# Mixture-of-experts down products with the two bf16 halves of an expert's inner activations side by side

## The chip, the cores and the metric
The kernel runs on one core of one Trainium2 chip. The metric is device microseconds of that core for one launch. TensorE is called PE here, its weight loads PEld, VectorE DVE, ScalarE ACT, GpSimd POOL and SyncE SP.

## The reference
Two transformer-like blocks run on 512 tokens of width 1024. The first has a gated linear attention and a state-space mixer, and then product-key retrieval of experts. The second has a token mixer with attention, and then a hierarchical mixture of experts. Only the last part is touched here:

```
x_rows = hf[row_tok]                       # rows sorted by expert, 32 experts, top 2 of them a token
a = xb @ w_e_gate[e]                       # 1024 -> 512
u = xb @ w_e_up[e]                         # 1024 -> 512
y = (silu(a) * u) @ w_e_down[e]            # 512 -> 1024
out = x + sum over a token's two experts of y * weight, then rmsnorm
```

## The kernel before, in words
All weights stream from HBM in float32 chunks of 128 x 2048 (1 MB). Each chunk is split in two bf16 parts: ACT copies it to `w_hi` (`hi_of`, line 1686), and DVE subtracts that from the original into `w_lo` (`lo_of`, line 2369). Activations are split in the same way. A product is then three bf16 matmuls, high by high, high by low and low by high, summed in PSUM (`mm3`, lines 738 to 740).

The mixture of experts takes up to 64 rows (`CAP`) of each of 32 experts. An expert has six chunks: two for gate, two for up, two for down. `w_hi` and `w_lo` are rings of four chunks; the float32 chunks wait in a ring of twelve, which SP loads. On PE each chunk costs 12 matmuls of 512 columns. The program of an engine for one expert is its `step`, run in a loop of two steps; each engine works through its own list strictly in order, and semaphores tie the lists together. In step c:

- **PE**: gate of expert c (24 matmuls), transposes of expert c-1's inner activations (`expert_hidden`, line 1275, 8 small matmuls), transposes of the gathered rows of c+1 (`expert_rows`, line 1245, 16 small matmuls), down of c-1 (24 matmuls with 64 columns of weights in the array), up of c (24 matmuls).
- **ACT**: high part of the inner activations of c-1 (line 1699), one `hi_of`, Silu of the gate sums (line 1695), copy of the transposed inner activations out of PSUM (line 1703), copy of the high half of the transposed rows (line 1690), three `hi_of`, copy of the down sums (line 1708), two `hi_of`.
- **DVE**: low part of the inner activations of c-1 (line 2460), two `lo_of`, copy of the low half of the transposed rows (line 2451), three `lo_of`, Silu times up (line 2456), one `lo_of`.
- **POOL** gathers the rows of a later expert by indirect DMA and stores the outputs of c-1 to HBM.

The chunk of `hi_of(k + 4)`, the first that ACT splits after its copies, is the first chunk of up; the next one is up's second. Before a chunk may be split, PE must be done with the chunk four places earlier. After the last expert, POOL gathers every token's two output rows, and DVE and ACT weigh, add and normalise them.

Of the kernel before, what the change touches and what calls it, by code (L numbers as in the profile page):

```python
# [11 lines left out]
ALU = mybir.AluOpType  # L12
# [141 lines left out]
def build_program(nc, w_all, x_in, cols_in, small_in, rows_in, out):  # L154
    ctx = ExitStack()
    with ctx:  # L156
# [3 lines left out]
        def sem(name):  # L160
            return ctx.enter_context(nc.semaphore(name))
# [163 lines left out]
        hid_b = view(o, 2, DE, dt=BF16); o += DE  # L325
        hidT = view(o, 2, DE // P, CAP, dt=BF16); o += DE // P * CAP
        y_st = view(o, 2, D); o += 2 * D
# [101 lines left out]
        xe_ld = [sem(f"xe_ld{p}") for p in range(2)]  # L429
        xe_tp, xe_hi, xe_lo = sem("xe_tp"), sem("xe_hi"), sem("xe_lo")  # L430
        moe_ld = w_ld + [sem(f"moe_ld{s}") for s in range(RING, MOE_RING // 2)]
        moe_mm = sem("moe_mm")
        sil_done, hid_mul, hid_hi, hid_lo, hid_tp, hid_c = (sem(n) for n in ("sil_done", "hid_mul", "hid_hi", "hid_lo", "hid_tp", "hid_c"))
        y_out = sem("y_out")
        y_stored = [sem(f"y_stored{p}") for p in range(2)]
# [297 lines left out]
        def _(pe):  # L733
# [504 lines left out]
            def expert_rows(r, i, c):  # L1238

                pe.wait_ge(xe_ld[c % 2], 16 * (pairs_of(r, i, c) + 1))  # L1240
                wait(pe, xe_hi, moe(r, i, c))
                wait(pe, xe_lo, moe(r, i, c))
                for a in range(2):
                    for kt in range(KT):
                        last = pe.matmul(ps[:, 6 + a, kt * CAP:(kt + 1) * CAP], x_g[0:CAP, c % 2, a, kt * P:(kt + 1) * P],
                                         ident_b[0:CAP, 0:CAP], start=True, stop=True)
                    last.then_inc(xe_tp, 1)

            def expert_in(r, i, c, k, bank):

                for part in range(2):
                    chunk(C_MOE + r * PASS + 12 * i + (k + part))
                    for j in range(4):
                        kt, w = part * 4 + j, slice(j * DE, (j + 1) * DE)
                        last = mm3(ps[0:CAP, bank, :], xeT[:, c % 2, 0, kt, :], xeT[:, c % 2, 1, kt, :],
                                   w_hi[:, (k + part) % RING, w], w_lo[:, (k + part) % RING, w], kt == 0, kt == KT - 1)
                    last.then_inc(moe_mm, 1)

            def expert_gate(r, i, c):
                wait(pe, sil_done, moe(r, i, c))  # L1260
                pe.wait_ge(xe_hi, moe(r, i, c) + 1)
                pe.wait_ge(xe_lo, moe(r, i, c) + 1)
                expert_in(r, i, c, 6 * c - 2 if c else 0, 0)

# [4 lines left out]
            def expert_hidden(r, i, c):  # L1269

                pe.wait_ge(hid_lo, moe(r, i, c) + 1)
                for a in range(2):
                    for f in range(DE // P):
                        n = a * (DE // P) + f
                        last = pe.matmul(ps[:, 4, n * CAP:(n + 1) * CAP], hid_b[0:CAP, a, f * P:(f + 1) * P], ident_b[0:CAP, 0:CAP],
                                         start=True, stop=True)
                last.then_inc(hid_tp, 1)

            def expert_down(r, i, c, k):
                pe.wait_ge(hid_c, moe(r, i, c) + 1)  # L1280
                pe.wait_ge(y_out, moe(r, i, c) + 1)
                for part in range(2):
                    chunk(C_MOE + r * PASS + 12 * i + (k + part))
                    for half in range(2):
                        for j in range(2):
                            f, w = part * 2 + j, slice(j * D + half * 512, j * D + (half + 1) * 512)
                            last = mm3(ps[0:CAP, 2 + half, :], hidT[:, 0, f, :], hidT[:, 1, f, :],
                                       w_hi[:, (k + part) % RING, w], w_lo[:, (k + part) % RING, w], f == 0, f == DE // P - 1)
                    last.then_inc(moe_mm, 1)
# [12 lines left out]
            def step(r, i, c, more=True):  # L1302
                expert_gate(r, i, c)
                expert_hidden(r, i, c - 1)
                if more:
                    expert_rows(r, i, c + 1)
                expert_down(r, i, c - 1, 6 * c)
                expert_up(r, i, c)
# [12 lines left out]
        def _(act):  # L1321
# [365 lines left out]

            def rows_hi(r, i, c):
                act.wait_ge(xe_tp, 2 * moe(r, i, c) + 5)
                act.activation(xeT[:, c % 2, 0, :, :].rearrange("p k t -> p (k t)"), ps[:, 6, 0:KT * CAP], ACT.Copy).then_inc(xe_hi, 1)  # L1690

# [9 lines left out]
            def hidden_copy(r, i, c):  # L1701
                act.wait_ge(hid_tp, moe(r, i, c) + 1)
                act.activation(hidT.rearrange("p a f t -> p (a f t)"), ps[:, 4, 0:2 * DE // P * CAP], ACT.Copy).then_inc(hid_c, 1)  # L1703

            def outputs(r, i, c, k):
                act.wait_ge(moe_mm, r * PASS + 12 * i + (k + 2 + RING))
                act.wait_ge(y_stored[c % 2], 16 * (pairs_of(r, i, c) + 1))
                act.activation(y_st[0:CAP, c % 2, :].rearrange("p (b n) -> p b n", b=2), ps[0:CAP, 2:4, :], ACT.Copy).then_inc(y_out, 1)  # L1708

            def first(r):  # L1710
                if not isinstance(r, int):
                    for k in range(AHEAD):
                        hi_of(r, 0, k)
                rows_hi(r, 0, 0)
                hi_of(r, 0, 3)
                hi_of(r, 0, 4)
                silu(r, 0, 0, 0)
                rows_hi(r, 0, 1)
                hi_of(r, 0, 5)
                hi_of(r, 0, 6)  # L1720

            def step(r, i, c, more=True):
                k = 6 * c - 2
                hidden_hi(r, i, c - 1)
                hi_of(r, i, k + 3)
                silu(r, i, c, k)
                hidden_copy(r, i, c - 1)
                if more:
                    rows_hi(r, i, c + 1)
                hi_of(r, i, k + 4)  # L1730
# [27 lines left out]
        def _(dve):  # L1758
# [689 lines left out]

            def rows_lo(r, i, c):
                dve.wait_ge(xe_tp, 2 * moe(r, i, c) + 6)  # L2450
                dve.tensor_copy(xeT[:, c % 2, 1, :, :].rearrange("p k t -> p (k t)"), ps[:, 7, 0:KT * CAP]).then_inc(xe_lo, 1)

# [9 lines left out]
            def first(r):  # L2462
# [6 lines left out]
                lo_of(r, 0, 1)  # L2469
                rows_lo(r, 0, 0)  # L2470
                for k in range(2, 5):
                    lo_of(r, 0, k)
                rows_lo(r, 0, 1)
                lo_of(r, 0, 5)
# [3 lines left out]
            def step(r, i, c, more=True):  # L2478
# [3 lines left out]
                lo_of(r, i, k + 4)  # L2482
                if more:
                    rows_lo(r, i, c + 1)
                lo_of(r, i, k + 5)
                lo_of(r, i, k + 6)
                if more:
                    lo_of(r, i, k + 7)
# [3 lines left out]
            def last(r):  # L2492
                step(r, 0, NE - 1, more=False)
                hidden_lo(r, 0, NE - 1)

            one_pass = every_expert(first, step, last)
# [111 lines left out]
```

## Time and profile before

| | |
|---|---|
| median of 3 runs | 2748.45 us (2743.22 to 2752.5) |
| profiled execution | 2750.43 us |
| its span | 2748.8 us |
| mean granted clock of PE | 0.981 |
| PE busy | 2609.0 us, 95% |
| DVE busy | 1941.9 us, 71% |
| ACT busy | 1230.8 us, 45% |
| DMA, mean over the span | 224 GB/s |
| a weight load into `xn`, issue to landing, median of 32 | 9.2 us |

A matmul's busy time in the profile overlaps that of the next one, so the distance from start to start is what it costs. The same holds for the short ACT and DVE instructions: the next one starts about 0.1 us before the one before is shown to end. The step of one expert is best read as the distance between the same instruction of two neighbouring experts.

### The profile page before, as it was taken

Reading aid. Unit: us, or ns where it says so; the run is one execution under the profiler, and the core shown is the slowest. Engines: PE = TensorE matmul, PEld = TensorE weight load, DVE = VectorE, ACT = ScalarE, POOL = GpSimd, SP = SyncE. Lnnn points to the kernel's source line nnn. Section 1 sums busy time; section 2 is a strip of 40 time slices with the busy share of each in tenths; the row PEclk is TensorE's granted clock in tenths of the full one; section 3 lists DMA queues with packets and bytes.
Section 4 is the critical chain, followed back from the end, with each engine's and each line's share of the span. In section 5 each row is a group of like instructions: output and inputs, shape, how many; then the busy total and the mean of one; then the engine's idle time right before and its main releaser. Section 6 shows DMA issues by size and latency. Waiting matters only on the chain. (4 is left out here: it accounts for less than half of the span.)

```text
span 2748.8 us, 38654 instructions
## 1 busy us (share of the span) xinstructions
PE 2609.0 (95%) x13878; PEld 1321.1 (48%) x14069; DVE 1941.9 (71%) x3255; ACT 1230.8 (45%) x1316; POOL 945.4 (34%) x724
## 2 busy tenths in 40 slices
PE   8989999999999999999999899999999799999994
PEld 4465444444444444444444444555544455555552
DVE  6455887988855635888888754465534688888885
ACT  5434223223234432333333443444422588888883
POOL 0000000277777736888888200000001322222221
PEclk9989999999999999999999999999999799999997
DMA  5201874343436478999999532211123699999993
GB/s 215 108 16 58 291 279 177 125 160 139 176 142 162 154 188 286 365 367 363 368 366 363 195 123 107 82 72 62 62 77 138 244 391 395 394 393 394 403 408 139
DMA packets 175580, 614.83 MB, mean 224 GB/s; under 512 B 58336, under 2 KB 74720, under 8 KB 125792
## 3 DMA queue, kind: packets, MB, share of 16 engines
q1 hardware_dynamic: 57312, 411.62, 39.5%
q0 software_dynamic: 47712, 127.12, 12.7%
q10 hardware_dynamic: 70432, 74.46, 8.8%
q8 instruction: 76, 1.25, 0.2%
q14 instruction: 48, 0.39, 0.0%
HBM read 539.59 MB, written 73.53 MB: 223 GB/s over the span
## 5 line engine op out<-in xcount | busy, mean ns | idle before, releaser
L739 PE MATMUL ps<-a_lo,w_hi 128*128 128x512 bf16 (+2 forms) x1747 | 642.2, 370 | 4.2 <-issue 0.8
L740 PE MATMUL ps<-a_hi,w_lo 128*128 128x512 bf16 (+2 forms) x1745 | 641.4, 370 | 1.3 <-DVE xn L2314 0.2
L738 PE MATMUL ps<-a_hi,w_hi 128*128 128x512 bf16 (+2 forms) x1698 | 623.4, 370 | 9.1 <-ACT xn L1492 3.0
L738 PE MATMUL ps<-w_hi,arena 128*128 128x512 bf16 (+1 forms) x1582 | 604.1, 382 | 26.6 <-ACT arena L1703 14.6
L739 PE MATMUL ps<-w_lo,arena 128*128 128x512 bf16 (+1 forms) x1583 | 603.7, 381 | 0.9
L740 PE MATMUL ps<-w_hi,arena 128*128 128x512 bf16 (+1 forms) x1583 | 603.2, 381 | 0.9
L2019 DVE TENSOR_TENSOR w_lo<-w_st,w_hi 128x2048 bf16<-128x2048 f32 x127 | 290.5, 2289 | 222.3 <-ACT w_hi L1486 222.3
L1486 ACT ACTIVATE w_hi<-w_st 128x2048 bf16<-128x2048 f32 x127 | 242.4, 1908 | 338.4 <-PE ps L740 317.9
L624 POOL DMA_INDIRECT gate_dram<-arena x256 | 320.4, 1252 | 85.4 <-issue 79.4
L1492 ACT ACTIVATE xn<-ps 128x512 f32<-128x512 f32 x128 | 76.1, 596 | 440.9 <-PE ps L740 440.9
L738 PEld LDWEIGHTS ps<-a_hi,w_hi 128*128 128x128 bf16 x1768 | 173.5, 98 | 195.0 <-issue 10.9
L740 PEld LDWEIGHTS ps<-a_hi,w_lo 128*128 128x128 bf16 x1768 | 173.4, 98 | 194.7 <-issue 1.8
L738 PEld LDWEIGHTS ps<-w_hi,arena 128*128 128x128 bf16 (+1 forms) x1600 | 166.6, 104 | 208.5 <-issue 19.4
L639 POOL DMA_INDIRECT arena<-act_dram,h_idx x128 | 248.7, 1943 | 39.0 <-issue 39.0
L739 PEld LDWEIGHTS ps<-a_lo,w_hi 128*128 128x128 bf16 x1768 | 173.3, 98 | 181.7 <-issue 1.1
L740 PEld LDWEIGHTS ps<-w_hi,arena 128*128 128x128 bf16 (+1 forms) x1600 | 166.7, 104 | 181.6 <-issue 3.7
L739 PEld LDWEIGHTS ps<-w_lo,arena 128*128 128x128 bf16 (+1 forms) x1600 | 166.6, 104 | 176.8 <-issue 2.9
L1767 DVE TENSOR_TENSOR w_lo<-w_st,w_hi 128x2048 bf16<-128x2048 f32 x68 | 155.0, 2287 | 121.7 <-ACT w_hi L1330 121.5
L667 POOL CAST arena<-xn 128x1024 bf16<-128x1024 f32 x4 | 4.1, 1036 | 549.4 <-DVE xn L1781 549.4
L1330 ACT ACTIVATE w_hi<-w_st 128x2048 bf16<-128x2048 f32 x68 | 129.0, 1906 | 99.3 <-PE ps L740 98.0
L2369 DVE TENSOR_TENSOR w_lo<-w_st,w_hi 128x2048 bf16<-128x2048 f32 x64 | 146.0, 2282 | 28.1 <-ACT w_hi L1686 28.1
L689 POOL DMA_DIRECT2D y_dram<-arena x32 | 18.3, 573 | 389.5 <-ACT arena L1708 389.5
(406 smaller groups left out, 3803.5 us busy)
## 6 DMA issues: line engine op xcount, KB each, us to landing
w_st<-in_w_all SPq DMA_DIRECT2D x260, 1024.0 KB, 5.5
arena<-in_w_all SPq DMA_DIRECT2D x64, 1024.0 KB, 9.5
act_dram<-xn POOLq DMA_DIRECT2D x64, 512.0 KB, 3.0
xn<-in_w_all SPq DMA_DIRECT2D x32, 1024.0 KB, 9.2
arena<-act_dram ACTq DMA_DIRECT2D x64, 384.0 KB, 5.3
gate_dram<-xn ACTq DMA_DIRECT2D x14, 1536.0 KB, 8.4
arena<-gate_dram ACTq DMA_DIRECT2D x64, 336.0 KB, 7.2
a_hi<-in_w_all SPq DMA_DIRECT2D x16, 1024.0 KB, 8.9
```

What stands on the lines that cost most here:

```text
L624: pool.indirect_dma_start(gate_cells, bass.IndirectOffsetOnAxis(ap=place[:, b, j:j + 1], axis=0), shared[:, b, j:j + 1], None).then_inc(g_ ...
L639: pool.indirect_dma_start(act_0[:, k:k + 1], None, acts, bass.IndirectOffsetOnAxis(ap=h_idx[:, k:k + 1], axis=0)).then_inc(act_ld[k // ROW ...
L689: pool.dma_start(y_dram[moe(r, i, c)], y_st[0:CAP, c % 2, :]).then_inc(y_stored[c % 2], 16)
L738: pe.matmul(dst, l_hi, r_hi, start=start, stop=False)
L739: pe.matmul(dst, l_hi, r_lo, start=False, stop=False)
L740: return pe.matmul(dst, l_lo, r_hi, start=False, stop=stop)
L1330: act.activation(dst, w_st[:, n % RING, :], ACT.Copy).then_inc(w_hi_done, 1)
L1486: act.activation(w_hi[:, s, :], w_st[:, s, :], ACT.Copy).then_inc(w_hi_done, 1)
L1492: act.activation(u_st[:, n % 2, t, :], ps[:, t, :], ACT.Gelu).then_inc(u_out, 1)
L1767: dve.tensor_tensor(lo_n, w_st[:, n % RING, :], hi_n, ALU.subtract).then_inc(w_lo_done, 1)
L2019: dve.tensor_tensor(w_lo[:, s, :], w_st[:, s, :], w_hi[:, s, :], ALU.subtract).then_inc(w_lo_done, 1)
L2369: dve.tensor_tensor(w_lo[:, s, :], moe_st[k % MOE_RING], w_hi[:, s, :], ALU.subtract).then_inc(w_lo_done, 1)
```

## The change
The transposed inner activations `hidT` are laid out with the high and the low half of a block of 128 features side by side, 2 x 64 columns. One matmul with all 128 columns as weights and `w_hi` as the moving side gives high by high in PSUM partitions 0 to 63 and low by high in partitions 64 to 127. A second one with the high half alone and `w_lo` adds the third product to partitions 0 to 63. So a down chunk has 8 matmuls and no longer 12. ACT then copies partitions 64 to 127 to SBUF (`outputs`), and DVE adds partitions 0 to 63 to them (`outputs_add`, new, between its fourth and fifth `lo_of`).

The transposes of expert c-1's inner activations move on PE from behind the gate product of c to a place within it, ahead of its last three matmuls. On ACT their copy moves ahead of Silu. The two halves of the transposed rows, which ACT and DVE copied one each, are now copied by ACT in one instruction of 1024 columns (`rows_out`), which waits for all 16 transposes.

```diff
-            def expert_in(r, i, c, k, bank):
+            def expert_in(r, i, c, k, bank, within=None):
...
+                        if within and kt == KT - 1:
+                            within()
                         last = mm3(ps[0:CAP, bank, :], xeT[:, c % 2, 0, kt, :], xeT[:, c % 2, 1, kt, :],
...
# expert_hidden
-                        n = a * (DE // P) + f
+                        n = 2 * f + a
...
# expert_down
-                            last = mm3(ps[0:CAP, 2 + half, :], hidT[:, 0, f, :], hidT[:, 1, f, :],
-                                       w_hi[:, (k + part) % RING, w], w_lo[:, (k + part) % RING, w], f == 0, f == DE // P - 1)
+                            both = lambda start, stop: pe.matmul(ps[0:2 * CAP, 2 + half, :], hidT[:, f, :, :].rearrange("p a t -> p (a t)"),
+                                                                 w_hi[:, (k + part) % RING, w], start=start, stop=stop)
+                            rest = lambda: pe.matmul(ps[0:CAP, 2 + half, :], hidT[:, f, 0, :], w_lo[:, (k + part) % RING, w],
+                                                     start=False, stop=False)
+                            if f < DE // P - 1:
+                                both(f == 0, False)
+                                last = rest()
+                            else:
+                                rest()
+                                last = both(False, True)
...
# PE's step
-                expert_gate(r, i, c)
-                expert_hidden(r, i, c - 1)
+                expert_gate(r, i, c, lambda: expert_hidden(r, i, c - 1))
...
# ACT
-            def rows_hi(r, i, c):
-                act.wait_ge(xe_tp, 2 * moe(r, i, c) + 5)
-                act.activation(xeT[:, c % 2, 0, :, :].rearrange("p k t -> p (k t)"), ps[:, 6, 0:KT * CAP], ACT.Copy).then_inc(xe_hi, 1)
+            def rows_out(r, i, c):
+                act.wait_ge(xe_tp, 2 * moe(r, i, c) + 6)
+                act.activation(xeT[:, c % 2, :, :, :].rearrange("p a k t -> p a (k t)"), ps[:, 6:8, 0:KT * CAP], ACT.Copy).then_inc(xe_done, 1)
...
-                act.activation(y_st[0:CAP, c % 2, :].rearrange("p (b n) -> p b n", b=2), ps[0:CAP, 2:4, :], ACT.Copy).then_inc(y_out, 1)
+                act.activation(y_st[0:CAP, c % 2, :].rearrange("p (b n) -> p b n", b=2), ps[CAP:2 * CAP, 2:4, :], ACT.Copy).then_inc(y_low, 1)
...
# ACT's step
                 hi_of(r, i, k + 3)
+                hidden_copy(r, i, c - 1)
                 silu(r, i, c, k)
-                hidden_copy(r, i, c - 1)
                 if more:
-                    rows_hi(r, i, c + 1)
+                    rows_out(r, i, c + 1)
...
# DVE
-            def rows_lo(r, i, c):
-                dve.wait_ge(xe_tp, 2 * moe(r, i, c) + 6)
-                dve.tensor_copy(xeT[:, c % 2, 1, :, :].rearrange("p k t -> p (k t)"), ps[:, 7, 0:KT * CAP]).then_inc(xe_lo, 1)
+            def outputs_add(r, i, c):
+                dve.wait_ge(y_low, moe(r, i, c) + 1)
+                y = y_st[0:CAP, c % 2, :].rearrange("p (b n) -> p b n", b=2)
+                dve.tensor_tensor(y, ps[0:CAP, 2:4, :], y, ALU.add).then_inc(y_out, 1)
...
# DVE's step
                 hidden_lo(r, i, c - 1)
                 lo_of(r, i, k + 3)
                 lo_of(r, i, k + 4)
-                if more:
-                    rows_lo(r, i, c + 1)
                 lo_of(r, i, k + 5)
                 lo_of(r, i, k + 6)
+                outputs_add(r, i, c - 1)
                 if more:
                     lo_of(r, i, k + 7)
                 hidden(r, i, c, k + 4)
```

## Rows read from the trace of the kernel before

**Rows 1.** Busy time by stretch; columns: us, then each engine, PEclk, DMA share, GB/s.
```profile
2400.00:2500.00 100.00, 97.40 (x569) 50.69 (x568) 88.77 (x53) 83.32 (x66) 28.03 (x19) 1.00 1.01 393
```

**Rows 2.** Waits, 2200 to 2650 us; columns: us in total, times, longest us.
```profile
DVE w_lo L2369 <- ACT w_hi L1686: 50.5, 27, 1.9
```

**Rows 3.** Timeline of PE, one step; columns: start us, us, operation [idle before <-releaser].
```profile
2640.51 0.38 PE L740 MATMUL ps<-w_hi,arena 128*64 128x512 bf16 x1
2640.82 0.41 PE L1275 MATMUL ps<-ident_b,arena 64*128 64x64 bf16 x8
2641.06 0.63 PE L1245 MATMUL ps<-ident_b,arena 64*128 64x64 bf16 x16
2642.12 0.40 PE L738 MATMUL ps<-w_hi,arena 128*64 128x512 bf16 x1 [0.43 <-ACT arena L1703]
...
2659.08 0.40 PE L738 MATMUL ps<-w_hi,arena 128*64 128x512 bf16 x1 [0.43 <-ACT arena L1703]
```

**Rows 4.** Timeline of DVE, the same step.
```profile
2639.55 0.68 DVE L2460 TENSOR_TENSOR arena<-arena 64x512 bf16<-64x512 f32 x1
...
2644.30 2.29 DVE L2369 TENSOR_TENSOR w_lo<-w_st,w_hi 128x2048 bf16<-128x2048 f32 x1 [1.87 <-ACT w_hi L1686]
2646.51 0.69 DVE L2451 CAST arena<-ps 128x512 bf16<-128x512 f32 x1
2647.11 2.28 DVE L2369 TENSOR_TENSOR w_lo<-w_st,w_hi 128x2048 bf16<-128x2048 f32 x1
...
2653.72 0.67 DVE L2456 TENSOR_TENSOR arena<-arena,ps 64x512 f32<-64x512 f32 x1
2654.31 2.28 DVE L2369 TENSOR_TENSOR w_lo<-arena,w_hi 128x2048 bf16<-128x2048 f32 x1
2656.51 0.67 DVE L2460 TENSOR_TENSOR arena<-arena 64x512 bf16<-64x512 f32 x1
```

**Rows 5.** Timeline of ACT, the same step.
```profile
2640.92 0.59 ACT L1695 ACTIVATE arena<-ps 64x512 f32<-64x512 f32 x1 [1.03 <-PE ps L740]
2641.41 0.58 ACT L1703 ACTIVATE arena<-ps 128x512 bf16<-128x512 f32 x1
...
2642.37 3.70 ACT L1686 ACTIVATE w_hi<-w_st 128x2048 bf16<-128x2048 f32 x2
...
2647.77 1.01 ACT L1708 ACTIVATE arena<-ps 64x1024 f32<-64x1024 f32 x1
2648.67 1.91 ACT L1686 ACTIVATE w_hi<-arena 128x2048 bf16<-128x2048 f32 x1
```

**Rows 6.** Timeline of PE, the last expert.
```profile
2707.18 0.41 PE L1275 MATMUL ps<-ident_b,arena 64*128 64x64 bf16 x8 [3.65 <-DVE arena L2460]
2708.27 0.63 PE L738 MATMUL ps<-w_hi,arena 128*64 128x512 bf16 x1 [0.69 <-ACT arena L1703]
```

**Rows 7.** Timeline of DVE, the last expert.
```profile
2706.45 0.68 DVE L2460 TENSOR_TENSOR arena<-arena 64x512 bf16<-64x512 f32 x1
```

**Rows 8.** Timeline of ACT: expert 1's Silu, expert 31's, and the last output copy.
```profile
2183.01 0.59 ACT L1695 ACTIVATE arena<-ps 64x512 f32<-64x512 f32 x1 [1.97 <-PE ps L740]
...
2691.86 0.59 ACT L1695 ACTIVATE arena<-ps 64x512 f32<-64x512 f32 x1 [1.09 <-PE ps L740]
...
2715.36 1.02 ACT L1708 ACTIVATE arena<-ps 64x1024 f32<-64x1024 f32 x1 [7.14 <-PE ps L740]
```

**Rows 9.** Timeline of SP's queue: the last weight loads.
```profile
2677.86 0.86 SPq L560 DMA_DIRECT2D xn<-in_w_all  x2
```

**Rows 10.** Timeline of PE, attention stage: two long waits.
```profile
1514.73 0.39 PE L738 MATMUL ps<-w_hi,arena 128*128 128x512 bf16 x1 [2.45 <-DVE arena L2169]
...
1544.68 0.59 PE L738 MATMUL ps<-w_hi,arena 128*128 128x512 bf16 x1 [3.88 <-DVE arena L2169]
```

**Rows 11.** Busy time by stretch, after each of those waits.
```profile
1514.00:1520.00 6.00, 5.22 (x24) 2.44 (x26) 5.82 (x6) 1.12 (x2) 4.78 (x5) 1.00 0.87 316
1544.00:1548.00 4.00, 3.32 (x9) 1.28 (x10) 3.10 (x3) 0.68 (x1) 0.00 (x0) 0.57 0.72 262
```

More of the change, by code:

```diff
@@ L325, in build_program @@
         hid_b = view(o, 2, DE, dt=BF16); o += DE
-        hidT = view(o, 2, DE // P, CAP, dt=BF16); o += DE // P * CAP
+        hidT = view(o, DE // P, 2, CAP, dt=BF16); o += DE // P * CAP
         y_st = view(o, 2, D); o += 2 * D
@@ L429, in build_program @@
         xe_ld = [sem(f"xe_ld{p}") for p in range(2)]
-        xe_tp, xe_hi, xe_lo = sem("xe_tp"), sem("xe_hi"), sem("xe_lo")
+        xe_tp, xe_done = sem("xe_tp"), sem("xe_done")
         moe_ld = w_ld + [sem(f"moe_ld{s}") for s in range(RING, MOE_RING // 2)]
@@ L433, in build_program @@
         sil_done, hid_mul, hid_hi, hid_lo, hid_tp, hid_c = (sem(n) for n in ("sil_done", "hid_mul", "hid_hi", "hid_lo", "hid_tp", "hid_c"))
-        y_out = sem("y_out")
+        y_low, y_out = sem("y_low"), sem("y_out")
         y_stored = [sem(f"y_stored{p}") for p in range(2)]
@@ L1240, in expert_rows @@
                 pe.wait_ge(xe_ld[c % 2], 16 * (pairs_of(r, i, c) + 1))
-                wait(pe, xe_hi, moe(r, i, c))
-                wait(pe, xe_lo, moe(r, i, c))
+                wait(pe, xe_done, moe(r, i, c))
                 for a in range(2):
@@ L1257, in expert_in, with expert_gate @@
                     last.then_inc(moe_mm, 1)
-            def expert_gate(r, i, c):
+            def expert_gate(r, i, c, within=None):
                 wait(pe, sil_done, moe(r, i, c))
-                pe.wait_ge(xe_hi, moe(r, i, c) + 1)
-                pe.wait_ge(xe_lo, moe(r, i, c) + 1)
-                expert_in(r, i, c, 6 * c - 2 if c else 0, 0)
+                pe.wait_ge(xe_done, moe(r, i, c) + 1)
+                expert_in(r, i, c, 6 * c - 2 if c else 0, 0, within)
             def expert_up(r, i, c):
@@ L1702, in hidden_copy @@
                 act.wait_ge(hid_tp, moe(r, i, c) + 1)
-                act.activation(hidT.rearrange("p a f t -> p (a f t)"), ps[:, 4, 0:2 * DE // P * CAP], ACT.Copy).then_inc(hid_c, 1)
+                act.activation(hidT.rearrange("p f a t -> p (f a t)"), ps[:, 4, 0:2 * DE // P * CAP], ACT.Copy).then_inc(hid_c, 1)
             def outputs(r, i, c, k):
@@ L1713, in first @@
                         hi_of(r, 0, k)
-                rows_hi(r, 0, 0)
+                rows_out(r, 0, 0)
                 hi_of(r, 0, 3)
@@ L1717, in first @@
                 silu(r, 0, 0, 0)
-                rows_hi(r, 0, 1)
+                rows_out(r, 0, 1)
                 hi_of(r, 0, 5)
@@ L2469, in first @@
                 lo_of(r, 0, 1)
-                rows_lo(r, 0, 0)
                 for k in range(2, 5):
                     lo_of(r, 0, k)
-                rows_lo(r, 0, 1)
                 lo_of(r, 0, 5)
@@ L2494, in last @@
                 hidden_lo(r, 0, NE - 1)
+                outputs_add(r, 0, NE - 1)
             one_pass = every_expert(first, step, last)
```

## The prediction

> **What bounds the kernel now.** I read the table of busy time by stretch first, to see what the stage of the experts is limited by. In any 100 us of it PE is busy for 97.4 us at full granted clock, DVE for 88.8, ACT for 83.3, and the DMA engines without a break at 393 GB/s [rows 1]. Four resources stand close together, so busy time alone decides nothing. Next the timeline of PE, for the length of a step: from the first down matmul of one expert to that of the next it is 2659.08 - 2642.12 = 16.96 us [rows 3]. Between the last gate matmul (2640.51) and the first down matmul (2642.12) lie 1.61 us. The other 71 distances of the 72 matmuls share 15.35 us, 0.216 us each. PE's only wait is the 0.43 us for ACT's copy of the transposed inner activations. PE bounds the step.
>
> The table of waits then shows that DVE has some slack of its own: 50.5 us in 27 steps, 1.87 us a step, in which it waits for ACT's split [rows 2, 4]. The last thing to read is who is nearly late. The low half of the inner activations (line 2460) starts on DVE at 2639.55 [rows 4]; PE's transposes of it start at 2640.82 [rows 3]. How long PE must wait at least after such a start is seen at the last expert, where PE really waited: 2706.45 on DVE, 2707.18 on PE, 0.73 us [rows 6, 7]. So PE could have started at 2640.28 and has 0.54 us in hand. The whole prediction turns on this number.
>
> **The change part by part, PE.** Eight down matmuls go: 8 x 0.216 = 1.73 us. The wait for the copy (0.43 us) is covered by the three gate matmuls and the row transposes. What is left on PE is 64 matmuls (13.8 us), the small transposes (2641.06 - 2640.82 = 0.24 us and 0.63 us) and about 0.2 us for changing between them: 14.9 us.
>
> **ACT.** Before: six splits, and copies that start 0.5 us apart (Silu 0.49, two copies up to 2642.37, so 0.48 each) [rows 5]. The two copies of 512 columns of rows become one of 1024. The nearest row is the copy of the down sums, 1024 columns in 2648.67 - 2647.77 = 0.90 us [rows 5]: ACT gains 0.42 us of work, and that ahead of the first split of up.
>
> **DVE.** It loses the copy of the rows, 2647.11 - 2646.51 = 0.60 us, and gets the sum of 1024 columns. Not shown in the trace, so bounded: 512 columns cost 2654.31 - 2653.72 = 0.59 us, twice that is 1.18; a split of 2048 columns costs 2.20, so a column costs (2.20 - 0.59) / 1536 = 1.05 ns and the sum 0.59 + 512 x 1.05 ns = 1.13 [rows 4]. I take 1.13. If the sum ran below the price of a column it could be 0.9, and if reading PSUM and SBUF at once hurts, 1.3.
>
> By these sums DVE would need 6 x 2.20 + 0.59 + 0.60 + 1.13 = 15.5 us and nobody 16.96. The step does get shorter if nothing else closes.
>
> **What closes.** The transposes of the inner activations now stand ahead of the last three gate matmuls. That is 3 x 0.216 = 0.65 us earlier, more than the 0.54 us in hand; and PE arrives earlier still, being faster elsewhere. So PE waits there for DVE's line 2460, with the end of the gate product queued behind it; Silu waits for that end; the copy of the rows waits too, as its transposes are behind it on PE; ACT's next split (first chunk of up) is queued behind both; DVE's split of the same chunk waits for ACT; and behind that, in DVE's own order, lie five more instructions before line 2460 comes round again. It is a ring, and I add it up from S, the start of line 2460:
>
> - S + 0.73: the eight transposes start on PE [rows 6, 7].
> - S + 0.97: the first of the three matmuls (0.24 for the transposes); the third starts at 1.43 (two distances of 0.22 to 0.24).
> - S + 1.84: Silu starts, 0.41 after the last gate matmul (2640.92 - 2640.51) [rows 3, 5]. It frees ACT at 2.33.
> - S + 1.74 to 2.37: the 16 row transposes (0.31 after the last gate matmul as 2640.82 - 2640.51, then 0.63) [rows 3]. The row copy starts at 2.40 and frees ACT at 3.30.
> - S + 5.23: DVE's split of up's first chunk, 2644.30 - 2642.37 = 1.93 after ACT's [rows 4, 5].
> - From there to line 2460 DVE took 2656.51 - 2644.30 = 12.21 us without a gap [rows 4]. Less 0.60, more 1.13: 12.74.
>
> The ring is 5.23 + 12.74 = 17.97 us, **1.01 us longer than the step now**. The sum waits for nobody: ACT's copy of the low half comes behind three splits (3.30 + 3 x 1.80 = 8.7, done at 9.6), and DVE reaches the sum at 5.23 + 6.61 = 11.8. Up's end is not late either: it needs the first split chunk at 7.4, then 24 matmuls, done near 12.9, and DVE comes to Silu times up at 15.1. PE stands still twice a step, about 1.3 us ahead of the transposes and 1.5 us ahead of up. The transfers, at 17 us a step of DMA time now, are not in the ring, and get slack.
>
> **The sum.** Silu of expert 1 starts at 2183.01 and that of expert 31 at 2691.86: 30 steps of 16.96 [rows 8]. 30 x 1.01 = +30.3. The first expert gets the longer row copy twice, partly behind the wait for rows: +0.3, estimated. At the end, from Silu of expert 31 to the end of the last copy, 2691.86 to 2716.38, is 24.52 us now [rows 8]. With the same pieces (no row copy; from S: Silu 1.84, split 4.26, sum done 12.0, Silu times up 12.6, last split 14.8, line 2460; transposes 0.73 on, down 1.09 after them [rows 6]; then the 7.09 us of now less 8 x 0.216 = 5.4; copy 1.02; sum 1.2) it becomes 22.4: -2.1. Total **+28.5 us**. The profiled execution would go from 2750.43 to 2778.9. That execution is 2.0 us over the median, so the median goes from 2748.45 to **2777**.
>
> **Rivals.**
>
> *The ring does not bind, and the transfers do (faster).* For it: no engine's own sum reaches 16.96, and the DMA engines are already without a break [rows 1], so they would be next. Place: the loads' queue. SP issues the last two weight loads at 2677.86 and 2678.4 [rows 9]; at 9.2 us they land near 2687.5. After that two splits (2 x 1.80 on ACT, 0.13 + 2.20 on DVE), eight matmuls and the copy (2.1 + 1.0) and the sum (1.2): near 2697.8, against 2716.4 now. At most 18.6 us are to be had, some 17 after imperfect packing: 2731 us. It decides as soon as the ring is under 16.96, which wants 1.0 us less than I find; against it, each link of the ring is a plain wait or the order of a list.
>
> *The ring and the step now come out even.* If several links are 0.2 us shorter than I read them, the step is 17 us or so, and the result within 8 us of before, 2748.
>
> *The granted clock falls in the two new waits (slower still).* In the attention stage a matmul that came after a wait of 2.45 us ran in 0.39 us, at a granted clock of 1.00, and one after 3.88 us in 0.59 us, at 0.57, that is partly at 1.2 GHz [rows 10, 11]. The new waits of 1.3 and 1.5 us are nearer to the first. If the clock fell in them all the same, the eight transposes and three matmuls in the ring would cost up to 0.24 + 0.65 = 0.9 us more, 27 us over the stage: 2804. The Trainium skill, TensorE: Matmul & The Clock Gate, section "HAM oscillation — how this bites in real kernels", says that waits that recur in each tile of a loop can let the clock drop to half each time. By that rule the result would be this rival's, by the row it is the forecast.
>
> **How the numbers follow.** Forecast 0.72, transfers 0.11, even 0.06, clock 0.07, the rest 0.04. The forecast's own spread: a step between 17.6 and 18.3 us (the sum 0.9 to 1.3 us, the row copy 0.8 to 1.06 us, 0.1 us for each change on PE), so 2766 to 2787; I take 2763 to 2790, which leaves a little under 2 in 10 outside. A measurement of this kernel tells about 0.3% (8 us) from no change. Faster by more than that: 0.13. Within: 0.04 (half of "even" falls a little to the slow side). Slower: 0.83.
>
> **What would show it.** The distance of two Silu starts on ACT (18.0, not under 17.2). On PE line 1275 preceded by an idle time of about 1.3 us, released by DVE line 2460, in each step. DVE without a gap from its split of up's first chunk to line 2460, and about 2.4 us idle ahead of that split (now 1.87). The new sum at 1.13 us a piece and without a wait. Granted clock 1.00 all through the stage. SP's loads waiting for free places in the ring and not for the loads before them, and the DMA share under 1. I am wrong if PE meets its transposes without a wait.

## The result, and the profile after

| | before | after |
|---|---|---|
| median | 2747.89 us (4 runs, 2743.22 to 2752.5) | 2787.11 us (4 runs, 2786.16 to 2788.66) |
| profiled execution, its span | 2750.43, 2748.8 us | 2786.16, 2784.4 us |
| step of one expert | 16.96 us | 18.11 us |

The changed kernel is slower: ratio 1.0135, 95% interval 1.012 to 1.015. Forecast were 2777 us, in a range of 2763 to 2790.

Busy time in a stretch of the stage (columns as in [rows 1]), after:

```profile
2400.00:2500.00 100.00, 90.08 (x482) 39.34 (x489) 85.10 (x49) 81.61 (x63) 42.12 (x16) 0.98 1.00 375
```

PE is busy for 90.08 us of 100 and not 97.4, the transfers fell from 393 to 375 GB/s, and DVE and ACT are no busier than they were. DVE's work for one expert, the step without its idle time, grew from 16.96 - 1.87 = 15.09 us to 18.11 - 2.48 = 15.63, and no engine's work reaches 18.11 us: PE's, without its waits of 1.23 and 0.34 us, is 16.5. So the step is set by waiting. The waits after, 2200 to 2690 us (us in total, times, longest):

```profile
DVE w_lo L2376 <- ACT w_hi L1693: 67.1, 27, 2.5
...
PE ps L1275 <- DVE arena L2468: 29.6, 24, 1.2
...
PE ps L738 <- DVE w_lo L2376: 8.0, 24, 0.3
```

PE waits for DVE's low half of the inner activations (line 2468, formerly 2460) 1.23 us a time in 24 recorded steps; before there was no such wait. Now one turn of the ring, in the order in which the prediction adds it up. DVE:

```profile
2635.25 0.68 DVE L2468 TENSOR_TENSOR arena<-arena 64x512 bf16<-64x512 f32 x1
...
2640.61 4.49 DVE L2376 TENSOR_TENSOR w_lo<-w_st,w_hi 128x2048 bf16<-128x2048 f32 x2 [2.48 <-ACT w_hi L1693]
...
2647.22 1.21 DVE L2459 TENSOR_TENSOR arena<-ps,arena 64x1024 f32<-64x1024 f32 x1
2648.36 2.27 DVE L2376 TENSOR_TENSOR w_lo<-arena,w_hi 128x2048 bf16<-128x2048 f32 x1
...
2653.36 0.68 DVE L2468 TENSOR_TENSOR arena<-arena 64x512 bf16<-64x512 f32 x1
```

Line 2468 starts at 2635.25 and again at 2653.36: **18.11 us** [rows 4 show 16.96]. From the split of up's first chunk (2640.61) to the next start DVE has no gap. Ahead of that split it is idle for 2.48 us. PE in the same turn:

```profile
2635.98 0.40 PE L1275 MATMUL ps<-ident_b,arena 64*128 64x64 bf16 x8 [1.23 <-DVE arena L2468]
2636.32 0.40 PE L738 MATMUL ps<-w_hi,arena 128*64 128x512 bf16 x1
2636.56 0.38 PE L739 MATMUL ps<-w_lo,arena 128*64 128x512 bf16 x1
2636.77 0.38 PE L740 MATMUL ps<-w_hi,arena 128*64 128x512 bf16 x1
2637.08 0.64 PE L1244 MATMUL ps<-ident_b,arena 64*128 64x64 bf16 x16
2637.97 0.40 PE L1289 MATMUL ps<-w_lo,arena 128*64 128x512 bf16 x1 [0.25 <-issue]
2638.31 0.39 PE L1287 MATMUL ps<-w_hi,arena 128*128 128x512 bf16 x1
2638.63 0.40 PE L1289 MATMUL ps<-w_lo,arena 128*64 128x512 bf16 x1
...
2642.96 0.40 PE L738 MATMUL ps<-w_hi,arena 128*64 128x512 bf16 x1 [0.34 <-DVE w_lo L2376]
```

The transposes start at 2635.98, 0.73 us after DVE's start, as at the last expert before [rows 6, 7]. The three gate matmuls follow at 2636.32, 2636.56 and 2636.77, and Silu only then, as ACT's timeline shows:

```profile
2637.19 0.59 ACT L1702 ACTIVATE arena<-ps 64x512 f32<-64x512 f32 x1 [0.17 <-PE ps L740]
2637.76 1.02 ACT L1697 ACTIVATE arena<-ps 128x1024 bf16<-128x1024 f32 x1
2638.68 3.70 ACT L1693 ACTIVATE w_hi<-w_st 128x2048 bf16<-128x2048 f32 x2
...
2655.30 0.59 ACT L1702 ACTIVATE arena<-ps 64x512 f32<-64x512 f32 x1 [0.17 <-PE ps L740]
...
2727.79 0.59 ACT L1702 ACTIVATE arena<-ps 64x512 f32<-64x512 f32 x1 [0.23 <-PE ps L740]
...
2750.48 1.02 ACT L1715 ACTIVATE arena<-ps 64x1024 f32<-64x1024 f32 x1 [7.80 <-PE ps L1287]
```

Silu 2637.19, row copy 2637.76, split 2638.68, and 1.93 us later DVE's split. Silu comes again at 2655.30, 18.11 us on; expert 31's comes at 2727.79, and the last output copy at 2750.48.

The gate matmuls are 0.22 to 0.24 us apart, but the down matmuls (lines 1287 and 1289 in turn) 0.32 to 0.34 us: 2637.97, 2638.31, 2638.63. The trace holds 15 of the 16: the first, of line 1287, is missing, and its place is the 0.25 us ahead of 2637.97. The recorded starts reach from 2637.97 to 2642.23; with 0.33 us for the missing one and 0.22 us for the last, sixteen take about 4.8 us, where 24 took 5.2 us. That was not foreseen: the prediction had 16 x 0.216 = 3.5 us.

### The profile page after: what moved, and what is told of

Its sections match the earlier page's. It is cut to its first block and busy times, and to the rows that moved or that the text cites. A ratio compares the mean times of both kernels' runs of the same rounds, so it can differ in the third digit from the quotient of the medians.

```text
span 2784.4 us, 38079 instructions
## 1 busy us (share of the span) xinstructions
PE 2603.9 (94%) x13590; PEld 1278.5 (46%) x13813; DVE 1958.6 (70%) x3255; ACT 1254.2 (45%) x1316; POOL 1028.6 (37%) x724
## 5 line engine op out<-in xcount | busy, mean ns | idle before, releaser
L738 PE MATMUL ps<-w_hi,arena 128*128 128x512 bf16 (+1 forms) x1326 | 506.5, 382 | 21.2 <-DVE arena L2176 10.1
L739 PE MATMUL ps<-w_lo,arena 128*128 128x512 bf16 (+1 forms) x1327 | 505.3, 381 | 0.9
L740 PE MATMUL ps<-w_hi,arena 128*128 128x512 bf16 (+1 forms) x1327 | 505.2, 381 | 0.9
L738 PEld LDWEIGHTS ps<-w_hi,arena 128*128 128x128 bf16 (+1 forms) x1344 | 137.9, 103 | 183.2 <-DVE w_lo L2376 23.9
L740 PEld LDWEIGHTS ps<-w_hi,arena 128*128 128x128 bf16 (+1 forms) x1344 | 138.2, 103 | 153.8 <-issue 2.8
L739 PEld LDWEIGHTS ps<-w_lo,arena 128*128 128x128 bf16 (+1 forms) x1344 | 138.2, 103 | 143.5 <-issue 2.4
L616 POOL DMA_DIRECT2D act_dram<-xn x64 | 35.9, 560 | 340.0 <-ACT xn L1499 322.8
```

The costliest lines, as they stand in the source:

```text
L616: pool.dma_start(act_dram[n], u_st[:, n % 2, :, :].rearrange("p j t -> p (j t)")).then_inc(u_stored[n % 2], 16)
L738: pe.matmul(dst, l_hi, r_hi, start=start, stop=False)
L739: pe.matmul(dst, l_hi, r_lo, start=False, stop=False)
L740: return pe.matmul(dst, l_lo, r_hi, start=False, stop=stop)
```

## The experiments

Theory A is the ring of the prediction. Each run had runs of the kernel before beside it on the same chip; ratios are to these. A step is the distance of two Silu starts of neighbouring experts in the trace. Two of the runs were single ones and have no ratio.

### The move undone

```diff
-                expert_gate(r, i, c, lambda: expert_hidden(r, i, c - 1))
+                expert_gate(r, i, c)
+                expert_hidden(r, i, c - 1)
...
-                hidden_copy(r, i, c - 1)
                 silu(r, i, c, k)
+                hidden_copy(r, i, c - 1)
```

> The changed kernel with one part undone: PE's transposes of the inner activations stand behind the gate product again, and ACT's copy of them behind Silu; the wide down products, DVE's sum and the row copy in one piece stay. Theory A (a ring: DVE's low half of the inner activations, PE's transposes, the last three gate matmuls, Silu, row copy, ACT's split, DVE's splits up to the low half again, 18.11 us): Silu no longer waits for the transposes, so the ring opens there; what remains long is the way through ACT's three copies to its split, about 17.4 us a step (distance of two Silu starts), some 2766 us. Rival B (the wide down products themselves set the step, since matmuls with 128 and with 64 columns of weights in turn are 0.33 us apart and not 0.216): the step stays near 18.1, 2787 us.

Measured: 2761.75 us, ratio 1.0045 (1.0029 to 1.006). Silu on ACT in two steps, and PE's wait for DVE's low half (us in total, times, longest, 2200 to 2680 us):

```profile
2598.67 0.59 ACT L1703 ACTIVATE arena<-ps 64x512 f32<-64x512 f32 x1
...
2615.93 0.59 ACT L1703 ACTIVATE arena<-ps 64x512 f32<-64x512 f32 x1
```

```profile
PE ps L1275 <- DVE arena L2469: 15.8, 27, 0.6
```

The step is 17.26 us, 0.15 under what was expected, and two thirds of the lost time are gone. The ring is shorter, not open: PE still waits 0.6 us a step for DVE's low half. Without the gate matmuls and Silu in it, the ring is 0.73 to the transposes, 0.44 to their copy on ACT, 0.49 to the row copy, 0.91 to the split, 1.94 to DVE's split and 12.75 back, together 17.26. With the rest of the change in place the move costs 0.85 us a step. This is not its price alone, as the move without the rest shows below. Rival B falls, for the down matmuls of 128 and 64 columns in turn are still there.

### Down matmuls grouped by width

```diff
...
+                    tiles = [(half, j) for half in range(2) for j in range(2)]
+                    if part == 0:
+                        for half, j in tiles:
+                            both(half, j, start=j == 0)
+                        for half, j in tiles:
+                            last = rest(half, j)
+                    else:
+                        for half, j in tiles:
+                            rest(half, j)
+                        for half, j in tiles:
+                            last = both(half, j, stop=j == 1)
...
```

(in place of the loops over `half` and `j` with one `both` and one `rest` each)

> The changed kernel with the 16 down matmuls of an expert in another order: per chunk the four with 128 columns of weights together and the four with 64 together, so that the width changes 3 times an expert and not 15 times. Theory C on the matmul distance (it is the change between the two widths that costs about 0.115 us each): distance 0.216 within a group, the down product falls from 4.5 to about 3.6 us, PE's stall behind it grows by as much. Rival (128-column weights behind a 64-column one are slow to load wherever they stand): still above 0.3. Theory A (ring): the step stays 18.1 us, since down is not in the ring, and only the last expert gains: 2785 us. Rival B (down product bounds the step): the step falls by 0.9 us, about 2760 us.

Measured: 2783.38 us, ratio 1.0132 (1.0098 to 1.0165). The down product on PE: three matmuls of 128 columns (the first of the four is missing in the trace, as before), eight of 64, four of 128.

```profile
2636.22 0.81 PE L1285 MATMUL ps<-w_hi,arena 128*128 128x512 bf16 x3 [0.16 <-issue]
2636.96 1.91 PE L1289 MATMUL ps<-w_lo,arena 128*64 128x512 bf16 x8
2638.81 1.04 PE L1285 MATMUL ps<-w_hi,arena 128*128 128x512 bf16 x4
```

Eight matmuls of 64 columns start and end within 1.91 us, so (1.91 - 0.38) / 7 = 0.22 us apart, and the four of 128 columns are as near to each other, (1.04 - 0.39) / 3 = 0.22: it is the change of width that costs 0.11 us, and not the wide weights. The expectation counts 15 changes an expert in the changed kernel; by its code and rows they are 12, since of the four blocks of features the last has its two matmuls in the other order. The down product is down from about 4.8 to about 3.7 us, and the step is still 18.11. What PE gained it now waits for the next split chunk:

```profile
PE ps L738 <- DVE w_lo L2382: 39.3, 27, 1.5
```

1.5 us a time, where it was 0.3. Down is off the ring, and a faster down product is worth nothing in the steps; at the last expert, where it is on the path, the kernel gained 2.2 us of the 24.96.

### One instruction of DVE moved

```diff
                 hidden(r, i, c, k + 4)
+                hidden_lo(r, i, c)
                 lo_of(r, i, k + 8 if more else k + 7)
```

(and taken away at the head of the step)

> The changed kernel with one instruction of DVE moved: the low half of the inner activations comes directly behind Silu times up, ahead of the step's last split and no longer behind it. Theory A (ring): the 2.2 us of that split leave the ring, the 0.7 us of waiting for ACT's high half come in: ring about 16.9 us or less; then the transfers come next (before the change they ran without a break at 17.0 to 17.2 us an expert), so a step of 16.9 to 17.2, 2750 to 2758 us. Rival B (wide down products, or DVE's total work, set the step): 18.1 as now or longer, since DVE now stands idle for 0.7 us more: 2787 to 2800 us.

Measured: 2749.18 us, ratio 1.0001 (0.9986 to 1.0016), step 16.91 us. The whole loss is gone with all parts of the change in place. DVE:

```profile
2621.30 0.67 DVE L2464 TENSOR_TENSOR arena<-arena,ps 64x512 f32<-64x512 f32 x1
2622.66 0.68 DVE L2468 TENSOR_TENSOR arena<-arena 64x512 bf16<-64x512 f32 x1 [0.69 <-ACT arena L1706]
...
2628.26 2.29 DVE L2376 TENSOR_TENSOR w_lo<-a_hi,w_hi 128x2048 bf16<-128x2048 f32 x1 [0.51 <-ACT w_hi L1693]
```

It now waits 0.69 us for ACT's high half, as reckoned, and only 0.51 and no longer 2.48 us for the split of up's first chunk. Giving DVE a new wait of 0.7 us made the kernel 38 us faster than the changed one: this is the plainest sign that order, and not work, was the bound.

The step of 16.91 us is again a ring, another one, and not the transfers that the expectation names. ACT in the same turn:

```profile
2622.00 0.63 ACT L1706 ACTIVATE arena<-arena 64x512 bf16<-64x512 f32 x1 [2.44 <-DVE arena L2464]
...
2626.33 1.90 ACT L1693 ACTIVATE w_hi<-a_hi 128x2048 bf16<-128x2048 f32 x1
```

From Silu times up on DVE (2621.30) it is 0.70 us to ACT's high half, 4.33 us through ACT's list without a wait to the split of up's first chunk, 1.93 us to DVE's split of it (2628.26), and 9.95 us through DVE's list without a gap to the next Silu times up (2638.21): 16.91.

### The move alone

The kernel before, with the transposes ahead of the last three gate matmuls and their copy ahead of Silu, and nothing else.

> The kernel before with only the move made: the transposes of the inner activations ahead of the last three gate matmuls on PE, their copy ahead of Silu on ACT; down products, row copies and DVE as before. Theory A (ring): the ring is closed here too, but with DVE's row copy of 0.60 us in place of the sum of 1.13, and with 0.48 us of row copy on ACT in place of 0.92: about 17.1 us a step, 2748 to 2754 us, so PE waits a little for DVE in each step. Rival B (the loss comes from the wide products): as before or faster by the 0.43 us wait a step that the move covers: 16.5 us, 2735 us.

Measured: 2751.7 us, ratio 1.0011 (1.0 to 1.0023), step 17.05 us. In the waits, PE for DVE's low half:

```profile
PE ps L1277 <- DVE arena L2461: 8.6, 28, 0.3
```

The ring closes here too, at 17.05, just over PE's 16.96. Covering the wait of 0.43 us brought nothing. Alone the move costs 0.09 us a step, and with the rest of the change 0.85: the two prices do not add up, since the move only costs as far as it makes the ring longer than the longest of the other bounds.

### The sum left out

```diff
-                act.activation(..., ps[CAP:2 * CAP, 2:4, :], ACT.Copy).then_inc(y_low, 1)
+                act.activation(..., ps[CAP:2 * CAP, 2:4, :], ACT.Copy).then_inc(y_out, 1)
...
-                outputs_add(r, i, c - 1)
```

(and the same behind the last expert)

> The changed kernel with DVE's sum of 1024 columns left out (only the low by high halves of the down products are stored). Theory A (ring): the 1.13 us of the sum leave the ring one for one, step 18.11 - 1.13 = 16.98 us, about 2751 us. Rival E (DVE has idle time in which the sum is hidden, 2.48 us a step): step stays 18.1, 2786 us.

Measured: one run, 2746.86 us; step 16.97 us. 18.11 - 16.97 = 1.14 us: the sum was in the ring with its full price, though DVE was idle for 2.48 us a step elsewhere. The other lengthened link, ACT's row copy of 0.92 us, is the one that no run takes out by itself.

### Was the kernel before held by its loads?

```diff
+                        n = CW if s < 8 else CW // 2
-                        sp.dma_start(moe_st[s], w_all[C_MOE + i * MOE_RING + s]).then_inc(moe_ld[s // 2], 16)
+                        sp.dma_start(moe_st[s][:, 0:n], w_all[C_MOE + i * MOE_RING + s][:, 0:n]).then_inc(moe_ld[s // 2], 16)
```

> The kernel before with the same lighter loads (half of the columns of 4 of 12 chunks not loaded). PE bounds it by the first reading: the step stays 16.96 us and the time 2748 us. If the loads, without a break, bounded it in truth: about 16 us, 2720 us.

Measured: one run, 2746.63 us, step 16.96 us. The loads carry 342 GB/s in it and not 400 (2500 to 2600 us), and SP's queue, which in the kernel before waits for nothing but earlier loads, mostly waits for free places. The step does not move at all, so the loads did not set it; that PE did rests on its timeline, with no wait but the 0.43 us.

### The ring taken apart

```diff
# PE and ACT: transposes behind gate, down matmuls grouped (as above)
# ACT
                 hi_of(r, i, k + 3)
+                hi_of(r, i, k + 4)
                 silu(r, i, c, k)
                 hidden_copy(r, i, c - 1)
                 if more:
                     rows_out(r, i, c + 1)
-                hi_of(r, i, k + 4)
                 hi_of(r, i, k + 5)
# DVE
                 hidden(r, i, c, k + 4)
+                outputs_add(r, i, c - 1)
+                hidden_lo(r, i, c)
                 lo_of(r, i, k + 8 if more else k + 7)
```

(and the two taken away at their old places)

> The changed kernel with its ring taken apart: transposes of the inner activations behind the gate product; down matmuls grouped by width of the weights; on DVE, directly behind Silu times up, first the sum of the previous expert (it covers the wait for ACT's high half) and then the low half; on ACT the split of up's first chunk ahead of Silu. Theory A: no ring is left above DVE's own work, 15.5 us a step; but then the transfers, without a break at 17.0 to 17.2 us an expert before the change, come next. The stage can end only about 10 to 13 us after the last load lands: 10 to 18 us less than before, 2732 to 2740 us, with steps of 15.5 us at first and about 17.1 once the lead of the loads is used up, and ACT waiting for loads. Rival D (transfers were not near their limit, they only follow the splits): 15.6 us all through, 2705 us. Rival B (the wide products set the step): 2785 us.

Measured: 2751.3 us, ratio 1.0014 (1.0005 to 1.0024); the trace is of the fastest of its 11 runs, 2746.24 us. An undisturbed step is 15.62 us (Silu at 2183.65, 2199.26 and 2214.88), DVE's own work as reckoned, but the next comes 18.13 us later, and so on. Neither theory named why. The waits from 2200 to 2680 us:

```profile
PE ps L1244 <- DMA arena<-x_dram,arena: 31.6, 12, 3.1
```

PE waits up to 3.1 us for gathered rows. POOL issues the gather behind the outputs' store and behind an index sum of 64 numbers, and that sum, 1.6 us in the kernel before and 3.8 in the changed one, takes 5.2 us on average here. POOL's timeline:

```profile
2469.39 0.57 POOL L689 DMA_DIRECT2D y_dram<-arena  x1 [10.03 <-DVE arena L2466]
2469.98 10.40 POOL L679 TENSOR_TENSOR arena<-arena,zero_i 64x1 int32<-64x1 int32 x1
```

10.40 us for 64 numbers, from 2469.98 to 2480.38. DVE ran splits without a gap from 2469.25 to 2482.6 then, and one of them ended at 2480.3, just ahead of the index sum.

> The kernel without the ring, and its weight loads lighter: of 4 of each 12 chunks only half of the columns are loaded (the rest keeps what an earlier load left there), a sixth of the bytes less; all splits and matmuls stay. Theory A (the transfers hold the kernel without the ring): the step falls to DVE's 15.6 us all through, about 2707 us. Rival D (they do not hold it): as the kernel without the ring.

Measured: 2738.54 us, ratio 0.9964 (0.9949 to 0.9979). 12.8 us faster than with full loads, but far from 2707: the waits for gathered rows are there as before (11 of them, 31.2 us). Both expectations miss; the late gathers hold this kernel in the main. Its runs spread from 2726.08 to 2747.86 us, and the trace is of the slowest, so what the lighter loads gained in the others is not shown.

### Gathers ahead of the store

The kernel with the ring taken apart, and in it:

```diff
# POOL
                 gather_next(r, 0, 2)
+                gather_next(r, 0, 3)
             def step(r, i, c):
-                gather_next(r, i, c + 2)
+                gather_next(r, i, c + 3)
                 store(r, i, c - 1)
             def last(r):
-                step(r, 0, NE - 3)
-                for e in range(NE - 3, NE):
+                for e in range(NE - 4, NE):
```

> The kernel without the ring showed steps of 15.62 us, broken in 12 of 28 steps by waits of PE of up to 3.1 us for the gathered rows. Its POOL issues a gather behind the store of an expert's outputs and behind an index sum of 64 numbers, which took 1.6 us before and 5.2 us there, up to 10.4, DVE being busy without a gap meanwhile. Here POOL's order is changed: the index sum and the gather come one expert earlier, ahead of that store. Theory F (the late gathers are what eats the gain): no waits of PE for gathered rows; steps of 15.6 us until the lead of the loads is used up, then about 17.1 set by the transfers with ACT waiting for loads; 2732 to 2740 us. Rival G (the transfers hold the kernel in either case, and the gathers only showed it): as without this change, 2745 to 2751 us.

> The same with the lighter weight loads (half of the columns of 4 of 12 chunks not loaded). Theory F: with neither the ring, nor late gathers, nor a full transfer queue, DVE's 15.6 us a step all through, 2705 to 2712 us. If POOL's index sum still waits for DVE, so that gathers are late again: waits of PE for gathered rows in some steps, 2725 us or more.

Measured with full loads: 2746.4 us, ratio 0.999 (0.998 to 0.9999), the only complete kernel of the study under the one before, by 0.1%, which is hardly more than nothing. With the lighter loads: 2713.75 us, ratio 0.9867 (0.9847 to 0.9886), steps of 15.63 us from the first to the last. The waits of PE for gathered rows are gone in both. With full loads the steps are 15.6 us up to 2312, and from 2400 on 17.0 to 17.7. Busy time at the beginning and in the middle:

```profile
2200.00:2300.00 100.00, 94.96 (x568) 47.11 (x574) 99.98 (x58) 92.80 (x72) 49.39 (x18) 1.00 1.01 395
...
2500.00:2600.00 100.00, 86.45 (x496) 41.86 (x500) 89.61 (x50) 83.15 (x64) 28.91 (x18) 0.97 1.02 390
```

DVE is at work for 99.98 us of 100 at first, then for 89.6: what ended its gaps is ACT, and ACT waits for the loads:

```profile
2601.49 1.91 ACT L1700 ACTIVATE w_hi<-w_st 128x2048 bf16<-128x2048 f32 x1 [1.06 <-DMA w_st<-in_w_all]
...
2623.88 1.91 ACT L1700 ACTIVATE w_hi<-a_hi 128x2048 bf16<-128x2048 f32 x1 [1.60 <-DMA a_lo<-in_w_all]
```

The same stretch with the lighter loads:

```profile
2500.00:2600.00 100.00, 94.93 (x567) 46.77 (x573) 99.96 (x58) 92.79 (x72) 51.14 (x19) 1.00 1.00 366
```

DVE has 99.96 us of work in 100, and ACT waits for no load. So the transfers come next once the ring and the late gathers are gone. The share of busy DMA engines does not tell this: it is about 1.0 in both, and ACT's waits for loads are there in one alone. By its time the kernel with full loads lies in the range of rival G (2745 to 2751), not in theory F's (2732 to 2740). What speaks for F is the order of the bounds: steps of 15.6 us first, then ACT waiting for loads, and 15.63 throughout with lighter loads. Its time was 6 us or more too good: the first Silu of the steady stretch comes at 2187.17, 4.2 us later than before, and at 17.0 to 17.7 the loads' steps are longer than the 17.1 assumed. With the lighter loads 2713.75 us is 1.75 over the top of the range.

## Why the prediction was right

**The ring** was predicted at 17.97 us and measured at 18.11. Link by link, from the start of DVE's line 2468: transposes 0.73 (predicted 0.73), third gate matmul 1.52 (1.43), Silu 1.94 (1.84), row copy 2.51 (2.40), its end 3.43 (3.30), DVE's split 5.36 (5.23), from there to the next start 12.75 (12.74). The reason is shown from four sides: undoing the move gives 17.26, moving DVE's instruction 16.91, leaving out the sum 16.97, the move alone 17.05. Grouping the down matmuls, outside the ring, leaves 18.11.

**The step that was mis-sized** is the first matmul after the transposes: "S + 0.97" was 1.07. I carried over the 0.24 us between two kinds of transposes with weights of the same shape, but here the shape changes from 64*128 to 128*64, and the distance is 0.34. The other way round, from the last gate matmul to the row transposes, it is 0.31 and not 0.22 (2636.77 to 2637.08); that the change of shape is the cause is likely by these rows, and not tested by itself. Thirty turns make 3 us of it; the ring's whole 0.14 us makes 4. The prediction had 0.1 us for each change on PE in its spread, not in its sum.

**The down product** was put at 16 x 0.216 us and is about 4.8 us, since each of its 12 changes of width costs 0.11 us. It is not in the ring and cost nothing in the steps: it only took from PE's wait ahead of up, which was predicted at 1.5 us and is 0.34, and 1.5 with the matmuls grouped. At the end it did cost: Silu of expert 31 to the end of the sum takes 24.96 us (2727.79 to 2752.75), predicted 22.4. PE, last expert:

```profile
2741.64 0.40 PE L1275 MATMUL ps<-ident_b,arena 64*128 64x64 bf16 x8 [3.65 <-DVE arena L2468]
2742.74 0.61 PE L1287 MATMUL ps<-w_hi,arena 128*128 128x512 bf16 x1 [0.69 <-ACT arena L1710]
2743.27 0.64 PE L1289 MATMUL ps<-w_lo,arena 128*64 128x512 bf16 x1
```

Between 2742.74 and the output copy at 2750.48 lie 7.74 us for 16 matmuls, where the prediction had 5.4; 24 took 7.09 before. Twelve changes of width are some 1.3 us of the difference of 2.3. The rest is the granted clock: in both kernels it is lower after the idle 3.65 us, but in the changed one for longer. The stretch from the transposes to the output copy, before and after:

```profile
2707.10:2715.40 8.30, 7.46 (x32) 3.35 (x32) 0.02 (x1) 0.64 (x2) 0.00 (x0) 0.79 0.01 3
...
2741.60:2750.50 8.90, 7.64 (x23) 1.86 (x24) 0.00 (x0) 0.62 (x2) 0.00 (x0) 0.62 0.02 4
```

Between its two levels, 1.2 and 2.4 GHz, the mean was 0.79 of full speed before and 0.62 after. The prediction took over the time of the kernel before with its share at the lower level; why it was longer stays open. With the matmuls grouped, Silu of expert 31 to the end of the sum took 22.7 us (2726.12 to 2748.87), near the 22.4 of the prediction; the granted clock there was 0.76 (2740 to 2747 us).

The Trainium skill has the rule that I had not weighed: TensorEngine Tiling (Array Packing), section "Key Properties", says that a change of the tiling mode drains the engine, while a change of tile within a mode does not. By that rule the alternation of 64 and 128 columns had to cost something; the trace agrees that it costs, with 0.11 us a change, and whether it is a drain no row shows.

**The start** was predicted at +0.3 us and is +1.45 (Silu of expert 1 at 2184.46, before 2183.01 [rows 8]). POOL's first gather:

```profile
2156.10 4.96 POOL L675 DMA_INDIRECT arena<-x_dram,arena  x1 [13.59 <-DVE arena L2474]
```

It took 4.96 us, and 2.76 before. Without the row copy on DVE two splits stand there one behind the other (2155.76 to 2160.23), and before it was one. The nine kernels without DVE's row copy show 4.96, the three with it 2.75 or 2.76. The rows came 1.65 us later, though the gather started 0.53 us earlier. Up to the first Silu 0.65 us of it were made good, and from there to expert 1's Silu 0.45 us were added, as much as the move alone adds (10.81 us for 10.36). The start of the first gather lies anywhere from 2152.28 to 2159.07 in the traces of the study, so that 1.45 us between two single executions is partly chance. I had looked for what the change adds on ACT and not for what it lets DVE do to POOL.

**The sum**: start +1.45, 30 steps of 1.15 us +34.5, end +0.44, what lies behind it (gathers of the outputs) -0.8: 35.6 us of span, predicted 28.5. The medians differ by 39.2 us; the 3.5 more is within the 9 us over which the kernel before spreads. So of the 10 us by which the median lies over the forecast, 4 are the ring's 0.14 us, 2.5 the end and 1 the start, 0.8 came back behind the last expert, and some 3 are the spread from run to run. The mechanism was right, and the range, whose upper end is 3 us away, had little room left.

**The signs.** PE's wait of 1.23 us ahead of the transposes (1.3 predicted), DVE's 2.48 us ahead of its split (2.4) and the sum's 1.14 us without a wait came as named. So did SP's change of reason. The waits of its queue, 2200 to 2600 us, the longest in total before and after:

```profile
SPq L559 <- DMA arena<-in_w_all: 96.6, 22, 6.2
...
SPq L560 <- DVE w_lo L2376: 226.8, 106, 3.9
```

Before, all of its waits are for earlier loads; after, most are for free places. The DMA share, which was to fall under 1, did not: it is 1.00 at 375 GB/s. A share of 1.00 does not show that the transfers hold a kernel, and neither does a queue of loads that waits for loads: the kernel before has both, and did not gain by lighter ones. What shows it is an engine that waits for a load, as ACT does with the gathers ahead of the store.

**The rivals.** Transfers as the bound did not come about, for the reason given against it. It was the right guess for what comes behind the ring, but it left out that POOL's gathers come between. The granted clock stayed at 0.98 to 1.00 over the stage in spite of two waits of about 1.2 and 0.3 us a step. The Trainium skill, TensorE: Matmul & The Clock Gate, section "HAM oscillation — how this bites in real kernels", tells of waits that recur and are several times as long. So its rule did not reach the waits here, and the prediction stretched it when it said that by that rule the result would be this rival's.

## What to carry to other kernels

Before an instruction is moved ahead on one engine, read by how much its input is early, in us, and compare that with the distance of the move: here 0.54 against 0.65, and the move alone made the step 0.09 us longer. Where the input is late, follow what is queued behind it all the way round until the same instruction comes again, and add up; if it is longer than every engine's own work, the sum is the new step, whatever the engines' busy shares say. And when a step is opened, look at the queue that nobody watches: a 64-number sum on POOL ended only when one of DVE's splits did, and its gathers came too late for PE.

## What the runs showed of the hardware that was not expected

- Matmuls of 512 columns with 128 and with 64 columns of weights in turn are 0.32 to 0.34 us apart, and 0.22 within a group of one width.
- A POOL instruction of 64 x 1 numbers takes 0.2 us when it starts outside of DVE's splits (at 2162.29 in the changed kernel). When it starts within a split, which has two inputs in SBUF, it ends 0.04 to 0.05 us behind the end of a split, in nearly every case from 2200 to 2660 us, in nine of the traces. That is the split then running for the kernel before (1.6 us) and the one with the moved instruction (0.98 us), the second one for the changed kernel (3.8 us), and the third to fifth in the long cases without the ring (6.0 to 10.4 us). How full DVE is does not set it: with DVE at work for 99.97 us of 100, it took 4.8 us on average in the last kernel, and 5.2 us with DVE at 90 to 95 in the one without the ring. The Trainium skill, SBUF — State Buffer, section "Who interferes with whom", says that a DVE instruction with two SBUF inputs contends with a GpSimd instruction that reads SBUF. The trace agrees, by these ends. Why it waits out several splits in one case and one in another stays open.
- A DVE sum of 64 x 1024 numbers with one input in PSUM and one in SBUF takes 1.13 to 1.14 us from start to start, less than twice the 0.60 of line 2464's 64 x 512 (2650.56 to 2651.16 in the changed kernel). This one was forecast, at 1.13, from the price of a column.
